# Two transformer layers in split fp32: ordered first loads, interleaved stage joins, and a VectorE tree for one sum of squares

## The reference, cut to what matters

```python
h = h + rmsnorm(mix, g_mix_post)                 # mix = (...) @ w_out          stage "out"
u = rmsnorm(h, g_ffn_pre)
up = causal_depthwise_conv(u @ w_up, conv_w, conv_b)                         #  stage "up"
gate_ff, value = jnp.split(up, [D_FF], axis=-1)
f = (gelu(gate_ff) * value) @ w_down                                         #  stage "down"
h = h + rmsnorm(f, g_ffn_post)
e = p @ w_ple_in                                                             #  stage "ple"
h = h + sigmoid(h @ w_ple_gate) * e                                          #  stage "ple_gate"
# second layer
proj = rmsnorm(h, attn_norm_g) @ w_in_2 + b_in_2                             #  stage "in2"
```

## Time and profile before

| | us |
|---|---|
| median of 3 runs | 2707.5 (2707.19 to 2707.92) |
| the profiled execution | 2707.43 |
| its span, first to last instruction | 2705.6 |
| TensorE busy | 2651.0 |
| VectorE busy | 1820.6 |
| ScalarE busy | 1303.6 |
| GpSimd busy | 327.2 |

### The profile page before, as it was taken

One profiled execution on the slowest core, in us unless ns is written; L12 is line 12 of the kernel. 1 busy time (PEld: TensorE's weight loads), 2 busy tenths in 40 slices (PEclk: granted clock), 3 DMA queues, 4 the chain that ended last, 5 costly groups with the idle time before them and its releaser, 6 DMA issues.

```text
span 2705.6 us, 57757 instructions
## 1 busy us (share of the span) xinstructions
PE 2651.0 (98%) x22838; PEld 2633.3 (97%) x22838; DVE 1820.6 (67%) x2327; ACT 1303.6 (48%) x1513; POOL 327.2 (12%) x325
## 2 busy tenths in 40 slices
PE   9999999997999999999999999999999999999998
PEld 9999999997999999999989999999999999999998
DVE  6555555746888888864466999957577776775444
ACT  5334454344555555444455444553465555554442
POOL 1000000032000000001101898600100000000000
PEclk9999999998999999999999999999999999999999
DMA  7665556563555555566655545556656656666664
GB/s 248 193 196 176 151 162 181 170 212 104 197 187 196 199 194 190 190 198 200 191 163 171 184 150 152 151 175 198 204 182 193 193 186 196 197 193 194 194 193 141
DMA packets 137803, 496.68 MB, mean 184 GB/s; under 512 B 15424, under 2 KB 15424, under 8 KB 137536
## 3 DMA queue, kind: packets, MB, share of 16 engines
q1 hardware_dynamic: 136800, 492.24, 58.3%
q10 hardware_dynamic: 864, 2.49, 0.2%
HBM read 492.57 MB, written 2.10 MB: 183 GB/s over the span
## 4 chain that ended last, share of the span: by engine, by line
PE 84%; DVE 8%; DVEq 4%; POOL 1%; issue 1%; ACT 1%; DMA 0%; POOLq 0%; SPq 0%; ACTq 0%
PE bank L414 82%; DVE w_lo L920 2%; PE ps_a L414 1%; DVE act_lo L959 1%; DVEq L1205 1%; DVEq L1246 0%; PE ps_o L414 0%; DVE hT L982 0%; DVE scn L1241 0%; ACT w_hi L651 0%; PE ps_n L414 0%; DVEq L1237 0%; DVEq L1216 0%; DVEq L1249 0%; DVE pr L1247 0%
## 5 line engine op out<-in xcount | busy, mean ns | idle before, releaser
L920 DVE TENSOR_TENSOR w_lo<-w_raw,w_hi 128x1024 fp32r<-128x1024 f32 x928 | 1133.0, 1235 | 720.2 <-ACT w_hi L651 719.0
L651 ACT ACTIVATE w_hi<-w_raw 128x1024 fp32r<-128x1024 f32 x928 | 976.0, 1055 | 1110.7 <-PE bank L414 1006.6
L414 PE MATMUL bank<-act_hi,w_hi 128*128 128x256 f32 x5536 | 1312.9, 279 | 22.4 <-DVE act_lo L959 15.8
L414 PE MATMUL bank<-act_lo,w_hi 128*128 128x256 f32 x5536 | 1301.6, 277 | 0.0
L414 PEld LDWEIGHTS bank<-act_hi,w_hi 128*128 128x128 f32 x5536 | 1043.7, 189 | 24.5 <-issue 17.5
L414 PEld LDWEIGHTS bank<-act_lo,w_hi 128*128 128x128 f32 x5536 | 1043.9, 189 | 0.7
L414 PE MATMUL bank<-act_hi,w_lo 128*128 128x256 f32 x5536 | 745.3, 277 | 7.5 <-DVE w_lo L920 7.5
L414 PEld LDWEIGHTS bank<-act_hi,w_lo 128*128 128x128 f32 x5536 | 683.8, 188 | 8.1 <-DVE w_lo L920 8.1
L414 PE MATMUL bank<-f_lo,w_hi 128*128 128x256 f32 x1408 | 327.9, 276 | 0.0
L414 PE MATMUL bank<-f_hi,w_hi 128*128 128x256 f32 x1408 | 327.8, 276 | 0.0
L414 PEld LDWEIGHTS bank<-f_hi,w_hi 128*128 128x128 f32 x1408 | 264.3, 188 | 0.0
(11 more groups left out here) (215 smaller groups left out, 1760.0 us busy)
## 6 DMA issues: line engine op xcount, KB each, us to landing
w_raw<-in_w_up SPq DMA_DIRECT2D x352, 512.0 KB, 4.2
w_raw<-in_w_in SPq DMA_DIRECT2D x252, 512.0 KB, 4.1
w_raw<-in_w_down SPq DMA_DIRECT2D x176, 512.0 KB, 4.3
w_raw<-in_w_out SPq DMA_DIRECT2D x64, 512.0 KB, 4.4
w_raw<-in_w_ple_gate SPq DMA_DIRECT2D x32, 512.0 KB, 4.7
w_raw<-in_w_branch_attn SPq DMA_DIRECT2D x16, 512.0 KB, 3.6
w_raw<-in_w_branch_a SPq DMA_DIRECT2D x8, 512.0 KB, 4.1
w_raw<-in_w_branch_b SPq DMA_DIRECT2D x8, 512.0 KB, 3.5
```

What stands on the lines that cost most here:

```text
L414: return pe.matmul(o, l, r, start=start, stop=stop, skip_group_check=True)
L651: act.activation(w_hi[:, k, 0:n, :], w_raw[:, k, 0:n, :], ACT.Copy).then_inc(hi_ready, 1)
L920: dve.tensor_tensor(w_lo[:, k, 0:n, :], w_raw[:, k, 0:n, :], w_hi[:, k, 0:n, :].bitcast(F32), ALU.subtract).then_inc(lo_ready, 1)
```

## The change

- Start: the first parameters go to SyncE's queue; ScalarE issues only chunk 0 of `hT`; SyncE issues chunks 1 to 3 behind the weight pieces 1 to 3, after a wait for chunk 0, then the other parameters. VectorE makes `w_lo` of piece 0 before the first `act_lo`.
- "up" gets the order `ACROSS`, spare banks, `hi_first`, two bodies written out, and its first three epilogues at pieces 13, 14 and 15. `w_hi` and `w_lo` of its first pieces are made before the norm (`ahead`). The first `normed` is cut in two. The squares are made by ScalarE into `eT` at pieces 7 and 8 and added by VectorE in a tree at pieces 8 and 9; GpSimd has no `add_squares(2)` any more; TensorE sums at piece 9 with 2 matmuls.
- "ple" is written out in full, its epilogues follow three pieces after their slot, the sum of squares moves from piece 1 to piece 0, the last three epilogues stand between the first pieces of "ple_gate". "ple_gate" gets `ACROSS` and `hi_first`.
- "in2" gets `ACROSS`, spare banks and `hi_first`; its first four `bc_pad` loads stand beside pieces 6 and 7.

```diff
@@ stages
+        st_up.crossed, st_up.spare, st_up.written_out, st_up.hi_first = ACROSS, ps_a, 2, 8
+        st_up.late = {13: [(0, 0)], 14: [(0, 1)], 15: [(1, 0)]}
+        st_ple.written_out, st_ple.late = 2, {g + 3: [(g // 4, g % 4)] for g in range(5)}
+        st_gate.crossed, st_gate.hi_first = ACROSS, 16
+        st_in2.crossed, st_in2.spare, st_in2.hi_first = ACROSS, ps_t, 24
@@ sync
+            sp.dma_start(par[:, 0:DT], a["params"][:, 0:DT]).then_inc(first_landed, 16)
-                    for m in which(lambda m: max(at_state(m) - 2, 0) if m >= STATE_RING else 2 + m, STATE_TILES, n):
+                    for m in which(lambda m: at_state(m) - 2 if m >= STATE_RING else 6 + m // 2, STATE_TILES, n):
+                        if st is st_in and first and 1 <= at < 4:
+                            if at == 1:
+                                sp.wait_ge(x_landed[0], 16)
+                            sp.dma_start(hT[:, 4 * at:4 * at + 4, :], a["xT"][:, 4 * at:4 * at + 4, :]
+                                         ).then_inc(x_landed[at], 16)
+                        if st is st_in and first and at == 3:
+                            sp.dma_start(par[:, DT:], a["params"][:, DT:]).then_inc(par_landed, 16)
@@ tensor
+                if n == 2:
+                    pe.wait_ge(quarters_added, 1)
+                    mm(ps_n[:, 0:TOK], ones, eT[:, 0, :], True, False)
+                    mm(ps_n[:, 0:TOK], ones, eT[:, 1, :], False, True).then_inc(sum_ready, 1)
+                    return
-                return lambda piece: sum_squares(n) if piece == {0: 7, 2: 5, 5: 5}[n] else None
+                return lambda piece: sum_squares(n) if piece == {0: 7, 2: 9, 5: 5}[n] else None
-            stream(st_ple, lambda piece: sum_squares(3) if piece == 1 else None)
+            stream(st_ple, lambda piece: sum_squares(3) if piece == 0 else None)
@@ scalar
+            ahead(st_up, range(3))
             last()
             root(1)
-            last = stream(st_up, gelu_gate(st_up, 0, ACT.Gelu_apprx_tanh), norm_beside(2))
+            ahead(st_up, (3,))
+            round_up(2, 0)
+            round_up(2, 1)
+            def beside_up(piece):
+                if piece in (5, 7):
+                    round_up(2, (piece - 1) // 2)
+                if piece in (7, 8):
+                    for c in (2 * piece - 14, 2 * piece - 13):
+                        x = slice(4 * c, 4 * c + 4)
+                        act.activation(eT[:, x, :], hT[:, x, :], ACT.Square).then_inc(quarter_squared, 1)
+                if piece == 13:
+                    root(2)
+            last = stream(st_up, gelu_gate(st_up, 0, ACT.Gelu_apprx_tanh), beside_up, ahead=4)
...
-            last = stream(st_ple, copy_to(st_ple, eT), lambda piece: root(3) if piece == 3 else None, last)
-            last()
+            ple_copy = copy_to(st_ple, eT)
+            stream(st_ple, ple_copy, lambda piece: root(3) if piece == 4 else None, last, 2)
+            round_up(3, 0)
+            for n in range(3):
+                ahead(st_gate, (n,))
+                ple_copy(1, n + 1)
+            round_up(3, 1)
+            ahead(st_gate, (3,))
...
-            last_ple = stream(st_gate, ple, lambda piece: round_up(3, piece) if piece < 4 else None)
+            last_ple = stream(st_gate, ple, lambda piece: round_up(3, piece - 2) if piece in (4, 5) else None, ahead=4)
@@ vector
+            ahead(st_in, (0,))
             round_off(0, 0)
...
+            ahead(st_up, range(3))
             root(1)
-            mixed(0)
-            mixed(1)
+            normed(mT, 0, 0, 2)
             round_off(2, 0)
-            last = stream(st_up, ffn(st_up, 0, "conv_w", "conv_b", 2 * FT, True), round_off_beside(2, mixed))
+            normed(mT, 0, 1)
+            ahead(st_up, (3,))
+            round_off(2, 1)
+            normed(mT, 0, 2)
+            def beside_up(piece):
+                if piece == 4:
+                    round_off(2, 2)
+                if piece == 5:
+                    normed(mT, 0, 3)
+                if piece == 6:
+                    round_off(2, 3)
+                if piece in (8, 9):
+                    c = 2 * (piece - 8)
+                    dve.wait_ge(quarter_squared, c + 2)
+                    dve.tensor_tensor(eT[:, 4 * c:4 * c + 4, :], eT[:, 4 * c:4 * c + 4, :],
+                                      eT[:, 4 * c + 4:4 * c + 8, :], ALU.add)
+                    dve.drain()
+                if piece == 9:
+                    dve.tensor_tensor(eT[:, 0:4, :], eT[:, 0:4, :], eT[:, 8:12, :], ALU.add)
+                    dve.drain()
+                    dve.tensor_tensor(eT[:, 0:2, :], eT[:, 0:2, :], eT[:, 2:4, :], ALU.add).then_inc(quarters_added, 1)
+                if piece == 13:
+                    root(2)
+            last = stream(st_up, ffn(st_up, 0, "conv_w", "conv_b", 2 * FT, True), beside_up, ahead=4)
...
+            def beside_ple(piece):
+                if piece == 4:
+                    root(3)
+                if piece == 6:
+                    fed(0)
+            stream(st_ple, None, beside_ple)
             round_off(3, 0)
-            last_ple = stream(st_gate, ple, round_off_beside(3, fed))
+            def beside_gate(piece):
+                if piece == 0:
+                    fed(1)
+                if piece == 1:
+                    round_off(3, 1)
+                if piece == 2:
+                    fed(2)
+                if piece == 3:
+                    round_off(3, 2)
+                    fed(3)
+                if piece == 5:
+                    round_off(3, 3)
+            last_ple = stream(st_gate, ple, beside_gate)
@@ gpsimd
             add_gained(1, mT, "g_mix_post", st_out)
-            add_squares(2)
```

More of the change, by code:

```diff
@@ L207, in build @@
         squares_of = lambda n: sq_t if n else sq_x[:, :, :]
+        pooled = lambda n: n - (n > 2)
         sq_slot = lambda n, k: squares_of(n)[:, 2 * k:2 * k + 2, :]
@@ L253, in build @@
         sum_ready, std_ready = sem("sum_ready"), sem("std_ready")
+        quarter_squared, quarters_added = sem("quarter_squared"), sem("quarters_added")
         gate_act = sem("gate_act")
@@ L842, in gelu_gate @@
                 return ep
-            act.dma_start(par[:, 0:DT], a["params"][:, 0:DT]).then_inc(first_landed, 16)
-            for c in range(4):
-                act.dma_start(hT[:, 4 * c:4 * c + 4, :], a["xT"][:, 4 * c:4 * c + 4, :]).then_inc(x_landed[c], 16)
-                if c == 0:
-                    act.preload_act_table(ACT.Sqrt)
-            act.dma_start(par[:, DT:], a["params"][:, DT:]).then_inc(par_landed, 16)
+            act.dma_start(hT[:, 0:4, :], a["xT"][:, 0:4, :]).then_inc(x_landed[0], 16)
+            act.preload_act_table(ACT.Sqrt)
             act.wait_ge(consts, 1)
@@ L973, in round_off_beside, with normed @@
                 return beside
-            def normed(src, n, c):
-                over = rstd[:, :].unsqueeze(1).to_broadcast([P, 4, TOK])
-                x = slice(4 * c, 4 * c + 4)
-                dve.wait_ge(gained, 8 * n + 2 * c + 2)
-                dve.tensor_tensor(tmp[:, c % 2, :, :], src[:, x, :], over, ALU.mult)
-                dve.drain()
-                dve.tensor_tensor(hT[:, x, :], hT[:, x, :], tmp[:, c % 2, :, :], ALU.add).then_inc(resid_ready, 2)
+            def normed(src, n, c, parts=1):
+                k = 4 // parts
+                over = rstd[:, :].unsqueeze(1).to_broadcast([P, k, TOK])
+                for at in range(0, 4, k):
+                    x, t = slice(4 * c + at, 4 * c + at + k), tmp[:, c % 2, at:at + k, :]
+                    dve.wait_ge(gained, 8 * n + 2 * c + (at + k) // 2)
+                    dve.tensor_tensor(t, src[:, x, :], over, ALU.mult)
+                    dve.drain()
+                    dve.tensor_tensor(hT[:, x, :], hT[:, x, :], t, ALU.add).then_inc(resid_ready, k // 2)
             def scaled_to(st, dst, pair0=0):
@@ L1350, in beside_in @@
                     root(0)
-            last = stream(st_in, scaled_to(st_in, proj1), beside_in)
+            last = stream(st_in, scaled_to(st_in, proj1), beside_in, ahead=1)
             dve.wait_ge(par_landed, 16)
@@ L1364, in _ @@
             stream(st_out, None, None, last, 0)
+            ahead(st_up, range(3))
             root(1)
-            def mixed(c):
-                normed(mT, 0, c)
-            mixed(0)
-            mixed(1)
+            normed(mT, 0, 0, 2)
             round_off(2, 0)
-            last = stream(st_up, ffn(st_up, 0, "conv_w", "conv_b", 2 * FT, True), round_off_beside(2, mixed))
+            normed(mT, 0, 1)
[17 more added lines that the diff above has]
+                    dve.tensor_tensor(eT[:, 0:4, :], eT[:, 0:4, :], eT[:, 8:12, :], ALU.add)
+                    dve.drain()
+                    dve.tensor_tensor(eT[:, 0:2, :], eT[:, 0:2, :], eT[:, 2:4, :], ALU.add).then_inc(quarters_added, 1)
+                if piece == 13:
+                    root(2)
```

(11 more changed lines are left out.)

12 lines of the change are left out of this document (6 added, 6 removed).

## The result

| us | before | after |
|---|---|---|
| median of the runs | 2707.57 (4 runs) | 2683.61 (2682.64 to 2684.16, 4 runs) |
| the profiled execution | 2707.43 | 2682.64 |
| its span | 2705.6 | 2680.7 |

The change makes the kernel faster by 24.0 us: ratio 0.9914, with a 95% interval of 0.9903 to 0.9926. The forecast was 2681.8. The two profiled executions are 24.8 us apart, against a forecast of 25.6.

A forecast was written before the change was run, and what follows sets the result against it. The prediction took TensorE's matmul pace as the bound, with time lost in four places besides the tail; 4.4 + 9.4 + 6.0 + 5.8 = 25.6 us off 2707.4 gave 2681.8 us, range 2674.5 to 2691.

The forecast's parts named there:

- the four places named: TensorE loses time at the start, out to up, ple and ple_gate, and gate to in2 with the mixer.
- Start: Kernel start: w_lo before act_lo lets TensorE run in full from 9.15 us; 4.4 us gained, range 2.5 to 4.7.
- The sum of 4.5: Kernel start: four pieces end at 20.0 instead of 24.6 us, put at 4.5 us gained, of which 4.4 taken.
- the added wait in SyncE's queue: Kernel start: SyncE waits for chunk 0 of hT; the fifth weight piece lands at 16.4, slack 2.5 us.
- Out to up: Between out and up: TensorE's loop starts at 681.7 instead of 691.1 us; 9.4 us gained, range 6.5 to 13.
- VectorE is now the longest chain. From 623.1: Out to up: VectorE's work sums to 57.0 us, freeing the seventeenth piece's bank at 680.1 us.
- Ple and ple_gate: From down's end to ple_gate's eighth piece: ple nearly without waits, ple_gate right behind; 6.0 us gained, range 4.5 to 7.5.
- Gate to in2: Gate to in2 and mixer: earlier fourth weight piece, VectorE's lead decides; 5.8 us gained, range 3.5 to 8.5.
- (1): TensorE keeps its lead, VectorE not the bound at up or in the mixer; 2673.5 us; chance 9%.
- (2): Half clock after new short waits at four or five places, or late chunks at the start; 2693 us; 17%.
- (3): VectorE falls behind in up's loop if its body lengthens by over 2.1 us; up to 2772 us; 3%.
- (4): Whole kernel: the waits only move and TensorE idles as long, later; within 5 us of before; 4%.

The follow-up runs named there:

- kernel 7: The changed kernel without VectorE's tree of adds, but for one tiny add that releases the sum; 2683.07 us.
- Kernels 6 and 9: The kernel before with only the bc_pad loads moved, 2701.44 us; and the changed kernel with in2's old matmul order and no spare banks, 2685.16 us.
- the tenth kernel: The changed kernel with the reciprocal and each epilogue one piece earlier in front of up's loop; 2685.1 us.
- The eighth kernel: The changed kernel with four spare banks instead of two for up's first slots, three bodies written out and its first epilogues spread; 2680.08 us.
- the third kernel: The changed kernel with ple and ple_gate put back as before; 2688.87 us.

## Why the prediction was right

The total is right to 1.8 us, and each of the four terms to within 0.9. They were not right to the same degree in their reasons, and with stretches that scatter by some 1.7 us, so close a fit of every term is in part luck.

**What bounds the kernel.** Right. The loss was in the four places named, and what a join saves stays saved: from the mixer's end on, the lead doesn't change (24.9 in both rows of the table).

**Start, forecast 4.4, measured 3.65.** The mechanism is right: `w_lo` before `act_lo`, no wait behind the zeros, full clock from the first real matmul.

```profile
9.01 1.29 PE L429 MATMUL ps_a<-act_hi,w_hi 128*128 128x256 f32 x8
10.14 1.07 PE L429 MATMUL ps_a<-act_hi,w_lo 128*128 128x256 f32 x8
```

Four pieces end at 20.3, where 20.0 was forecast, a lead of 4.3. At the ordinary bank 3.5 of it are left (3.65 at the end of out). The sum of 4.5 had no term for loads behind the fifth piece, and the seventh was a late one. It comes in the chain after as

```profile
15.01 9.09 DMA w_raw<-in_w_in
25.21 1.84 DVE w_lo L957
27.10 4.81 PE ps_a L429 x40
```

and it landed at 24.1, where ScalarE had waited 1.16 us for it and TensorE then 0.28. The fifth piece too was later than forecast, near 18.0 instead of 16.4, which cost nothing. The seventh's lateness doesn't come from the added wait in SyncE's queue, which the forecast had feared: before, without that wait, the same piece came at 24.66, and ScalarE waited 2.50 us for it:

```profile
24.66 1.06 ACT L651 ACTIVATE w_hi<-w_raw 128x1024 fp32r<-128x1024 f32 x1 [2.50 <-DMA w_raw<-in_w_in]
```

A TensorE that is 4 us ahead needs the piece sooner, and that term was left out. In both kernels the load of the tables (1152 KB) stands right in front of it; no run moved it. Pieces five to eight took 11.6 us instead of 11.2 before, and the sum of squares behind them 0.35 more.

**Out to up, forecast 9.4, measured 10.1.** The first wait was 4.92 us (forecast about 4.5), the two late ones 0.56 and 2.46 (forecast 2 and 3), the half clock behind them 1.7 us (charged 1.6): 5964 matmuls took 677.98 us, and at 0.1134 each they need 676.3. The bank of the seventeenth piece came free at 675.5; the forecast's 680.1 less the start's 3.65 is 676.45. The step that led there, "VectorE is now the longest chain. From 623.1", is right as a path: its 57.0 us measured 56.0 (619.48 to 675.5). It is wrong as a price list. A sum over one engine's work says nothing of the paths beside it, and I took each of its terms to be worth its length, as what I expected of kernel 7 shows for the tree's 4.6 us. Kernel 7 shows a second path, over VectorE's `w_lo` of piece 9, the load of piece 13 and ScalarE, that is only 0.5 us shorter up to the `w_lo` of piece 13; only behind that point is VectorE alone the bound. The forecast didn't look at that path, and it was luck that it wasn't the longer one. The sum would have misled anyone who went on to optimize by it.

**Ple and ple_gate, forecast 6.0, measured 5.7.** Ple_gate started at 1366.47, right behind ple, where TensorE stood 5.05 before. Two waits are left, both as named: 1.50 for an epilogue, 1.86 for the fifth piece's `w_lo` (forecast 1.5 and 1.7). I had charged 0.2 for clock; the 0.3 missing is of that size, and no row tells more.

**Gate to in2, forecast 5.8, measured 5.4.** Right in mechanism and in what is lost. TensorE was 8.2 us ahead of before at the eighth piece (forecast 8) and kept 5.4 of it; VectorE came to its reciprocal 5.4 us earlier, counted from the eighth piece of ple_gate (1476.91 - 1390.4 against 1501.81 - 1409.9; forecast 5.3). The 0.5 added for waits of VectorE for ScalarE in the mixer didn't come: the lead at the reciprocal and at the mixer's end are the same. Kernels 6 and 9 sharpen the step: the load's place in SyncE's queue is all of the gain, and the interleaved order, whose lead the forecast gave up as lost, has none that these runs can tell from nothing.

**The rivals.** (1) TensorE didn't keep its lead, at up or in the mixer. (2) More given back: part of it exists. In the trace of after, half clock fell behind the waits of 4.92 and 2.46 us at out to up and nowhere else between the start and the tail, two places and not five; other kernels show it behind waits of 1.4 and 1.8 us too. (3) In the loop of up VectorE's waits for `w_hi` are 43.5 us in 40 of them, against 41.5 in 39: the slack of 2.1 us per body is still there, so VectorE caught up at once. (4) The four kernels with a part undone exclude it.

```profile
DVE w_lo L957 <- ACT w_hi L671: 43.5, 40, 1.5
```

## What to carry to other kernels

When an engine waits for a chain of several engines, summing the work of one of them gives a time, but not what a cut in it is worth. Find the points at which that engine is *fed* (here a piece of weights whose load waits for a buffer that the engine itself gives back four pieces earlier), and compare the way round with the work: between two such points a cut gains only until the way round is the longer one, and behind the last of them it gains in full. And in a queue that issues in order, a load that waits for a result holds up every load behind it; moving one such line behind the loads that are needed first gained 6.1 us of stretch here (5.2 in the medians), as much as any rewriting of a stage but that of up.

## What the runs showed of the hardware

The same wait in front of the same matmuls sometimes costs clock and sometimes doesn't. At the fifth piece of ple_gate TensorE waits 1.86 us after the change and 1.81 in the tenth kernel, whose code there is the same. By stretch (columns as the earlier trace rows), first after, then the tenth kernel:

```profile
1380.33:1384.33 4.00, 4.00 (x35) 4.00 (x36) 4.00 (x4) 3.14 (x3) 0.00 (x0) 1.00 0.66 206
```

```profile
1380.96:1384.96 4.00, 4.00 (x21) 4.00 (x22) 4.00 (x4) 3.13 (x3) 0.00 (x0) 0.57 0.66 212
```

TensorE stays at 2.4 GHz in one and falls to 1.2 for most of 4 us in the other: 21 matmuls instead of 35, and the 568 matmuls from there take 66.55 us instead of 64.67. The eighth kernel falls there too (66.32). Behind the second layer's mixer it is the same with a wait of 1.4 us: 1512 matmuls take 171.6 to 171.7 us in seven of the fourteen traces and 173.2 to 173.3 in the other seven, with the same code. In the third kernel the row of that place is

```profile
1767.79:1784.79 17.00, 17.00 (x135) 17.00 (x136) 9.66 (x9) 11.12 (x16) 0.00 (x0) 0.90 0.58 177
```

The Trainium skill (TensorE: Matmul & The Clock Gate, What's actually happening) says of the matmuls at low clock at a kernel's start that their number varies between runs of one kernel. These rows fit that, and show it in the middle of a kernel too; but they compare kernels with the same code at that place, one trace each, and not runs of one kernel. Each such place is 1.3 to 1.9 us. Two or three of them with the start's own scatter would make up the 1.5 to 6.5 us by which the runs of one kernel differ here; that is an inference, since only one run of each kernel was traced. Such a place can lie inside a stretch as well: 1.9 and 1.7 us of it are in the tenth and the eighth kernel's 353.7 and 352.8 us from ple_gate to the mixer's end. Removing a wait of 1.4 to 2.5 us is therefore worth its length and sometimes up to 1.9 us more; what decides it, these runs don't show.
